# Forty-eight expert-routed tokens by indexed rows instead of thirty-two, in a transformer kernel that streams its weights

## The reference, cut to what matters

```
act = gelu(einsum('thkd,td->thk', u[ib], tb))
out = einsum('thk,thkd->td', gb * act, v[ib])      # u, v: 16384 x 2048
x   = x + out
```

## Time and profile before

| | |
|---|---|
| median of 3 runs (lowest, highest) | 3161.68 us (3159.88, 3164.09) |
| the profiled execution's own time | 3165.17 us |
| its span, first to last instruction | 3163.4 us |
| mean granted TensorE clock | 0.991 |

### The profile page before, as it was taken

The page is one execution under the profiler, slowest core; times in us unless marked ns, Lnnn a source line. Parts: engine busy times, 40 slices in busy tenths (PEclk is TensorE's granted clock), DMA queues, the critical chain, the costliest instruction groups (busy, mean ns, idle before and its releaser), DMA issues.

```text
span 3163.4 us, 49697 instructions
## 1 busy us (share of the span) xinstructions
PE 3065.3 (97%) x19428; PEld 2810.0 (89%) x19428; DVE 2239.1 (71%) x3268; ACT 1407.0 (44%) x1670; POOL 142.6 (5%) x168
## 2 busy tenths in 40 slices
PE   7999999999999999999999999999898999999998
PEld 7899889899999999999999999998787888888887
DVE  4766549998867888888888677687655646555564
ACT  4465443366434444444444445434444333333333
POOL 1000000000001101011111000000000000000000
PEclk9999999999999999999999999999999999999999
DMA  5443454456767888888888665544353555555553
GB/s 201 175 145 145 148 194 152 164 209 215 257 239 281 316 298 310 299 315 298 311 299 308 238 240 175 186 164 153 132 177 115 191 191 186 195 186 188 194 189 133
DMA packets 95836, 673.14 MB, mean 213 GB/s; under 512 B 11560, under 2 KB 11584, under 8 KB 15968
## 3 DMA queue, kind: packets, MB, share of 16 engines
q1 hardware_dynamic: 77472, 562.07, 49.2%
q0 software_dynamic: 16224, 94.72, 8.8%
q10 hardware_dynamic: 2016, 14.68, 1.2%
HBM read 652.48 MB, written 18.89 MB: 212 GB/s over the span
## 4 chain that ended last, share of the span: by engine, by line
PE 86%; DVE 10%; ACT 3%; issue 1%; DMA 0%; ACTq 0%; POOL 0%; DVEq 0%; SPq 0%
PE bank L1862 29%; PE bank L1863 15%; PE bank L1890 6%; PE bank L1892 6%; PE bank L1891 6%; PE bank L1840 6%; PE bank L1842 5%; PE bank L1841 5%; DVE w_lo L1085 4%; PE bank L1868 2%; ACT w_hi L653 1%; DVE pick_a L1502 1%; PE bank L1954 1%; PE bank L2154 1%; DVE tmp L1269 1%
## 5 line engine op out<-in xcount | busy, mean ns | idle before, releaser
L1085 DVE TENSOR_TENSOR w_lo<-raw,w_hi 128x2048 fp32r<-128x2048 f32 x532 | 1218.4, 2290 | 543.3 <-ACT w_hi L653 521.0
L1862 PE MATMUL bank<-a_both,w_hi 128*128 128x448 f32 (+1 forms) x3840 | 1259.1, 380 | 7.1 <-DVE a_both L1102 3.9
L1863 PE MATMUL bank<-a_both,w_lo 128*128 128x224 f32 (+1 forms) x4096 | 1060.8, 269 | 0.0
L1862 PEld LDWEIGHTS bank<-a_both,w_hi 128*128 128x128 f32 x3840 | 721.7, 188 | 90.6 <-DVE a_both L1102 4.4
L1863 PEld LDWEIGHTS bank<-a_both,w_lo 128*128 128x128 f32 x4096 | 778.5, 190 | 11.7
L653 ACT ACTIVATE w_hi<-raw 128x2048 fp32r<-128x2048 f32 x308 | 588.4, 1911 | 395.0 <-PE bank L1892 376.9
L1840 PE MATMUL bank<-a_both,w_hi 128*128 128x256 f32 (+1 forms) x1984 | 572.0, 288 | 21.2 <-DVE w_lo L1085 14.0
L666 ACT ACTIVATE w_hi<-raw 128x1536 fp32r<-128x1536 f32 x224 | 333.6, 1489 | 571.4 <-PE bank L1863 570.0
L1841 PE MATMUL bank<-a_both,w_hi 128*128 128x256 f32 (+1 forms) x1984 | 560.1, 282 | 0.0
L1842 PE MATMUL bank<-a_both,w_lo 128*128 128x256 f32 (+1 forms) x1984 | 559.9, 282 | 0.0
L1840 PEld LDWEIGHTS bank<-a_both,w_hi 128*128 128x128 f32 x1984 | 383.8, 193 | 28.8 <-issue 12.3
(11 more groups left out here) (326 smaller groups left out, 2442.0 us busy)
## 6 DMA issues: line engine op xcount, KB each, us to landing
raw<-stream_dram SPq DMA_DIRECT2D x532, 1024.0 KB
gates_scratch<-stage ACTq DMA_DIRECT2D x14, 1024.0 KB, 4.8
gbuf<-gates_scratch POOLq DMA_DIRECT2D x30, 448.0 KB, 7.0
x<-x_dram SPq DMA_DIRECT2D x2, 1024.0 KB, 6.6
x_scratch<-x POOLq DMA_DIRECT2D x1, 2048.0 KB, 11.0
wide<-wide_dram POOLq DMA_DIRECT2D x2, 1024.0 KB, 8.8
mem<-mem_dram POOLq DMA_DIRECT2D x1, 2048.0 KB, 9.5
xm<-x_scratch POOLq DMA_DIRECT2D x1, 2048.0 KB, 9.5
```

Source lines behind the costliest of these rows:

```text
L1085: eng.tensor_tensor(w_lo[k % SPLIT][:, :], raw[:, k % RAW, :], w_hi[k % SPLIT][:, :].bitcast(F32), ALU.subtract).then_inc(split_done, 1)
L1862: mm(o, hi[:, ks], pair, start=kt == 0, stop=False)
L1863: inst = mm(o2, lo[:, ks], pair[:, 0, :], start=False, stop=False, skip_group_check=True)
```

## The change: what it does

G becomes 48, in two sets: tokens 0 to 31 as before, and tokens 32 to 47 as eight groups of 16, so that 16 more tiles of each kind are fetched (`SETS`). The dense columns TD become 208, the gate groups 52, the gate blocks 13. There are 96 gathers and jobs in place of 64, 18 in a full round in place of 13, up to u7. The tokens' rows are multiplied by the norm's weights once, early (48 partitions, in the projection wq), stored to DRAM, and laid out for both sets by two DMAs. In rounds 2 to 7 the rounding of the gated product moves from DVE to ACT (`cast`), and the last piece of it on DVE (`act_lo`) is done one unit later. The second selection matmuls stand in e7, the norm of the memory input is later, and its tiles are turned at units 5 to 15 of e7, two at a time at first (`GMEM_AT`). The indices, gates and factors of the rows are laid out by 36 small DMAs in place of 12.

```diff
-G = 32
-GROUPS_G, GJ = P // G, PICKS // (P // G)
+SETS = [(0, 32), (32, 16)]
+G = GJ = sum(n for _, n in SETS)
+SET_DMAS = sum(P // n for _, n in SETS)
 TD = T - G
...
-        JOBS_U, JOBS_E = (1, 4, 7, 10, 13), tuple(range(0, 16, 2))
+        JOBS = {"u": (1, 3, 5, 6, 8, 10, 11, 13), "e": (0, 2, 3, 5, 6, 8, 10, 11, 13, 14)}
+        JOBS_FIRST = (3, 5, 6, 8, 9, 11, 12, 13)
+        JOBS_LAST = (1, 3, 5, 7, 9, 11)
...
+        GMEM_AT = {5 + j: (2 * j, 2 * j + 1) for j in range(5)}
+        GMEM_AT.update({10 + j: (10 + j,) for j in range(6)})
...
             eng.wait_ge(s_xd, 16)
+            eng.wait_ge(tr_done, TRQ["ln2"] + 16)
+            eng.dma_start(wide2[0:G, :], wide_in[2:3, :].partition_broadcast(G)).then_inc(s_wide2, 16)
+            eng.wait_ge(xw_done, 1)
+            eng.dma_start(xw_d, xw[0:G, :]).then_inc(s_xw, 16)
...
             gather(0)
-            eng.dma_start(wide2[:, :], wide_in[2:3, :].partition_broadcast(P)).then_inc(s_rows, 16)
+            gather(1)
             eng.wait_ge(mm_done, UNIT0["u2"])
-            for c in range(GROUPS_G):
-                eng.dma_start(h_rows[c * G:c * G + G, :], x_d[0:G, :]).then_inc(s_rows, 16)
-            eng.wait_ge(rows_done, 1)
-            gather(1)
+            for i, (t0, n) in enumerate(SETS):
+                src = bass.AP(tensor=xw_d.tensor, offset=t0 * D, ap=[[0, P // n], [D, n], [1, D]])
+                eng.dma_start(set_rows[i][:, :], src).then_inc(s_rows, 16)
...
+            def cast(r, k):
+                eng.wait_ge(g_used, 16 * r + k + 1)
+                eng.activation(a2[0][:, k, 0:TD], tmp[:, k % 4, 0:TD], ACT.Copy).then_inc(act_hi, 1)
...
                     eng.activation(tmp[:, j, 0:TD], tmp[:, j, 0:TD], ACT.Gelu).then_inc(tmp_full, 1)
+                    if k >= 1:
+                        cast(r, k - 1)
                     if k == 15:
                         ahead_rest(u)
+                        cast(r, 15)
...
+                if s == 2:
+                    eng.wait_ge(s_wide2, 16)
+                    eng.tensor_tensor(xw[0:G, :], x[0:G, 0, :], wide2[0:G, :], ALU.mult).then_inc(xw_done, 1)
...
-            def gating(r, k):
+            def gate_hidden(r, k):
...
-                own.do(eng.tensor_copy(a2[0][:, k, 0:TD], t))
-                eng.tensor_tensor(a2[1][:, k, 0:TD], t, a2[0][:, k, 0:TD].bitcast(F32), ALU.subtract).then_inc(tmp_split, 1)
+            def act_lo(r, k):
+                eng.wait_ge(act_hi, 16 * (r - 2) + k + 1)
+                eng.tensor_tensor(a2[1][:, k, 0:TD], tmp[:, k % 4, 0:TD], a2[0][:, k, 0:TD].bitcast(F32), ALU.subtract)\
+                    .then_inc(tmp_split, 1)
...
-                    gating(r, k)
+                    gate_hidden(r, k)
+                    if k > 0:
+                        act_lo(r, k - 1)
                     if k == 15:
+                        act_lo(r, 15)
                         ahead(UNIT0[f"u{r}"] + k)
-                    if (r, k) == (2, 1):
-                        eng.wait_ge(s_rows, 16 * (1 + GROUPS_G))
-                        eng.tensor_tensor(h_rows[:, :], h_rows[:, :], wide2[:, :], ALU.mult).then_inc(rows_done, 1)
...
             for j in range(16):
-                if j == 0:
-                    eng.wait_ge(sel_added, 1)
+                if j in (0, 1):
+                    sel_rows(1, j)
+                if j == 5:
+                    eng.wait_ge(sel_added, 2)
                     eng.wait_ge(normed, 4)
-                    turn_tile("gmem", mem, 0)
-                if j < 15:
-                    turn_tile("gmem", mem, j + 1)
+                for kt in GMEM_AT.get(j, ()):
+                    turn_tile("gmem", mem, kt)
```

More of the change, by code:

```diff
@@ L260, in build @@
         got = at("got", [P, 2, D], F32, work_at)
+        xw = at("xw", [P, D], F32, work_at)
         wide2 = at("wide2", [P, D], F32, work_at + 8192)
-        h_rows = at("h_rows", [P, D], F32, pk)
-        acc_rows = at("acc_rows", [P, D], F32, pk)
+        rows_at = work_at + 16384 + 4 * TBLOCKS * 4 * TBLOCK * 4
+        set_rows = [at(f"set_rows{i}", [P, D], F32, rows_at + 8192 * i) for i in range(len(SETS))]
+        assert rows_at + 8192 * len(SETS) <= work_at + WORK
         xm = at("xm", [P, TT, D], F32, work_at + 16384)
@@ L438, in build @@
         PART = 3 * UNIT // 4
-        JOBS_U, JOBS_E = (1, 4, 7, 10, 13), tuple(range(0, 16, 2))
+        JOBS = {"u": (1, 3, 5, 6, 8, 10, 11, 13), "e": (0, 2, 3, 5, 6, 8, 10, 11, 13, 14)}
+        JOBS_FIRST = (3, 5, 6, 8, 9, 11, 12, 13)
+        JOBS_LAST = (1, 3, 5, 7, 9, 11)
         JOB_AT, _n = {}, 0
-        for _r in range(2, PEER_ROUNDS - 1):
-            for _kind, _ks in (("u", JOBS_U), ("e", JOBS_E)):
-                for _k in _ks:
+        for _r in range(2, PEER_ROUNDS):
+            for _kind in "ue":
+                for _k in JOBS_LAST if _r == PEER_ROUNDS - 1 else JOBS_FIRST if (_kind, _r) == ("u", 2) else JOBS[_kind]:
                     if _n < 2 * GJ:
@@ L448, in build, with set_of @@
         assert _n == 2 * GJ
+        def set_of(j):
+            return next(i for i, (t0, n) in enumerate(SETS) if t0 <= j < t0 + n)
+        GMEM_AT = {5 + j: (2 * j, 2 * j + 1) for j in range(5)}
+        GMEM_AT.update({10 + j: (10 + j,) for j in range(6)})
         ROW_ACT_AT = next(at for at, n in JOB_AT.items() if n == GJ)
@@ L960, in _ @@
                 ahead_rest(UNIT0["e7"] + j)
+                if j < TT:
+                    eng.wait_ge(sel_done, 1)
+                    eng.wait_ge(s_mem, 16)
+                    square("gmem", mem, j)
             part_square(1, xm, 2)
@@ L1669, in _ @@
             for j in range(16):
-                if j == 0:
-                    scaled_lo("gmem", 0)
-                if j < 15:
-                    scaled_lo("gmem", j + 1)
+                for kt in GMEM_AT.get(j, ()):
+                    scaled_lo("gmem", kt)
                 accumulate(7, j)
                 ahead(UNIT0["e7"] + j)
+                if j == 2:
+                    sel_add(1)
+                    normalise("gmem", mem, mem)
                 if j in (6, 10, 14):
@@ L2179, in _, with sel_rows @@
                 feature("e2", 16, a2_both, r, unit=part_unit, rb=EB, c1=TD, ready=gated_tile("u2", r))
-            def sel_rows(h):
+            def sel_rows(i, h):
+                t0, n = SETS[i]
                 if h == 0:
-                    eng.wait_ge(got_used, 2 * GJ)
+                    eng.wait_ge(got_used, GJ + t0 + n)
                 for kt in range(8 * h, 8 * h + 8):
-                    last = mm(bank[4][:, kt * G:kt * G + G], acc_rows[:, kt * P:kt * P + P], C("sel"), start=True, stop=True)
+                    last = mm(bank[(4, 6)[i]][:, kt * n:kt * n + n], set_rows[i][:, kt * P:kt * P + P], C("sel", t0, t0 + n),
+                              start=True, stop=True)
                 if h == 1:
@@ L2403, in _constants @@
         np.broadcast_to(np.arange(P, dtype=np.float32), (P, P)),
-        (p % G == np.arange(G)[None, :]).astype(np.float32)], axis=1)
+        *[(p % n == np.arange(n)[None, :]).astype(np.float32) for _, n in SETS]], axis=1)
     onehot = np.zeros((BUCKETS, REL), np.float32)
```

90 lines of the change are left out of this document (48 added, 42 removed).

## The result

| | before | after |
|---|---|---|
| median us (lowest, highest) | 3161.86 (3159.88, 3164.09) | 3140.78 (3139.25, 3141.73) |
| ratio after / before, 95% interval | | 0.993 (0.9918 to 0.9942) |
| span of the profiled execution, mean granted clock | 3163.4, 0.991 | 3139.9, 0.989 |

A forecast was written before the change was run, and what follows sets the result against it. TensorE's own matmul sequence was taken as the bound, with VectorE and the DMAs next. 47.8 - 5.4 + 3.5 + 5.5 - 3.4 = 48.0 us saved, from 3161.7 to 3113.7 us (said as 3114), range 3090 to 3141.

The forecast's parts named there:

- The failed step: Small DMAs and row layouts: 24 more small DMAs and two layouts, issued while POOL is idle, were costed at nothing.
- such signs: Prediction wrong if the clock drops in the rounds or jobs wait for tiles; no w_hi was to wait for raw.
- Term 1, columns: In 224 units of e0, e1 and rounds 2 to 7, fewer w_hi columns save 47.8 us; w_lo sits at a floor.
- Term 2, VectorE: In rounds, TensorE waits for VectorE behind neighbouring jobs (3 us) and at changes from u to e (2.4): 5.4 lost.
- Term 3, the clock and the old stall: In u2, the 1.77 us wait for w_lo and 1.7 us lost at a lower clock go: 3.5 us saved.
- Term 4, gates: In u1, four groups fewer make units 11 and 12 shorter: 5.5 us saved, between 3 and 8.
- Term 5, selection: 16 more selection matmuls, two records each, 32 x 0.106: 3.4 us lost.
- the early multiplication: In wq, 2.2 us of VectorE falls into its idle 4.35 us: nothing; up to 5 if weights load late.
- 1 (no floor): In the matmul pairs all 48 columns count, giving 3090 to 3096 us; chance 0.2.
- 2 (the DMAs): In the rounds DMAs become the bound; at 340 GB/s sustained 30 us go back, 3144 us; chance 0.08.
- 3 (15 to 35 us given back by lag and late tiles): Longer VectorE lag, late tiles or the e7 shift give 15 to 35 us back, 3125 to 3150; chance 0.13.
- 4 (clock drop at every wait): In the rounds each wait throws the clock to its lower level, 66 us lost, 3175 us; chance 0.08.

The follow-up runs named there:

- e7: Not a run: a stage of the kernel, the e stage of round 7; 1.4 us longer in the changed kernel's trace than before.
- b_twelve: The changed kernel with the two row layouts loaded by twelve plain DMAs (four of 32 rows, eight of 16); 3124.2 us, ratio 0.9871.
- f_lo: b_twelve with the w_lo matmul taking only the first 104 of 208 columns in the 224 paired units; 3122.01 us, ratio 0.9873.
- f_hi: b_twelve with the w_hi matmul taking 400 of its 416 columns in the same 224 units; 3104.12 us, ratio 0.9815.
- c_copies: The changed kernel with multiplied rows written twelve times during wq, each layout then one DMA of 128 different rows; 3122.53 us, ratio 0.9878.
- m_wide0: The changed kernel with set 1 laid out by eight DMAs of 16 rows, set 0 still by one repeating DMA; 3148.4 us, ratio 0.9951.
- s_spaced: b_twelve with jobs moved to avoid neighbouring u units (7 in a u stage, 11 in an e stage); 3118.79 us, ratio 0.9862.
- v_cast: b_twelve with the rounding of the gated product back on VectorE, the subtraction directly behind it; 3131.74 us, ratio 0.9898.
- e6: Not a run: a stage of the kernel, the e stage of round 6; 1.9 us shorter in the changed kernel's trace than before.

## Why the prediction was wrong, point by point

**The failed step** is the sentence "the 24 more small DMAs and two row layouts are issued while POOL is idle", costed at nothing. It is true, and it prices the wrong thing: I looked at the queue that issues and not at the 16 engines that carry, nor at the first job, which waits for the layouts with a `w_lo` behind it. POOL was idle; the layouts then took 40.4 us, `w_hi` waited 14.5 us for the stream, VectorE 12.1 us for the rows, TensorE therefore 15.0 us for `w_lo`, and some 9.4 us went by at half the clock. The prediction had named such signs: the clock dropped in the rounds, `w_hi` waited for `raw`, and a job waited, though for its rows and not for its tile. b_twelve, which changes nothing else, gives 18.7 us back by the ratios and 17.7 by the spans, 19.6 of it in u2. The trace of before had no such DMA: its four loads of `h_rows` landed quickly, and one DMA with a leading repeat of 4 is another thing than four DMAs. That was to be bounded from both sides, and wasn't. The rest of the miss, 27 - 19 = 8 us, is spread over the small terms below. That 3140.8 lies just inside the stated range of 3090 to 3141 is luck: its high end was set for the DMA bound and for longer waits in all rounds, and neither came.

**Term 1, columns (47.8).** The number was nearly right, its reason was not. Pairs take 0.300 us, there are 1072 matmuls in the window of e0 and e1 (1067 said), and f_lo and f_hi show that the narrow matmul's columns are free and the wide one's are paid. But the prediction put the floor under the distance from `w_lo` to `w_hi`, and called itself wrong if that fell below 0.10: it fell from 0.101 to 0.095 in e1 (medians), the other distance from 0.212 to 0.205, and in f_lo it fell to 0.05. So neither the 0.106 us of the selection rows nor the 107 ns beside it is a floor for that distance; what the narrow matmul's columns hide behind is open. In u stages the unit stays near 4.85 us, not 4.80, 0.8 us a stage or 5 us over u2 to u7. That is in the traces; why is open. In u0, where I took nothing, it came out 0.9 us slower; in c_copies and m_wide0 it takes 96.8 us as before, so that comes and goes.

**Term 2, VectorE (-5.4).** Right in kind and place; the waits at the change from u to e have the predicted size, those behind neighbouring jobs a third of it. With a job VectorE's u unit took 5.50 us (5.57 said), its e unit 5.11 (5.15 said). The wait at the change from u3 to e3 (0.4 said):

```profile
1203.35 0.45 PE L1902 MATMUL bank<-a_both,w_hi 128*128 128x416 f32 x1 [0.34 <-DVE w_lo L1117]
```

There is one such at each change from u to e, 0.33 to 0.34 us long and 0.51 at e2, as the late subtraction makes it. Behind neighbouring jobs in u3 to u6 TensorE loses 0.11 us each time, in two pairs of 0.33 to 0.43 and 0.38 us instead of 0.30; 0.3 was said. The sum that gave 0.26 took 5.57 us twice, and twice 0.07 less leaves 0.12. s_spaced ends these; v_cast ends the waits at e3 to e6 and makes those behind neighbouring jobs 0.7 to 0.9 us long. Of b_twelve's two waits in the window 1100 to 1260 one, of 0.29 us, is of another kind: it stands behind a job of e2 whose tile came late:

```profile
1099.69 2.29 DVE L1635 CUSTOM_DVE_ANT_0 got<-got,set_rows 128x2048 f32<-128x2048 f32 x1 [1.16 <-DMA got<-u_rows_dram,row_idx]
```

Moving the cast is worth 8 us: without it VectorE would have been the next bound.

**Term 3, the clock and the old stall (+3.5)** can be judged by b_twelve alone, where u2 has neither: it takes 79.94 us, 5.3 less than before, where columns (3.4), stall (3.5) and waits (some -0.5) made 6.4. **Term 4, gates (+5.5):** u1 is 6.2 us shorter. Units 11 and 12 end 16.97 us after unit 10's, 15.1 said and 23.0 before:

```profile
757.96 0.34 ACT L927 ACTIVATE act<-bank 128x208 f32<-128x208 f32 x1 [0.19 <-PE bank L1882]
769.57 0.34 ACT L927 ACTIVATE act<-bank 128x208 f32<-128x208 f32 x1 [2.74 <-PE bank L1882]
774.93 0.34 ACT L927 ACTIVATE act<-bank 128x208 f32<-128x208 f32 x1 [3.21 <-PE bank L1882]
```

**Term 5, selection (-3.4):** the first set of 16 matmuls takes 1.70 us as before; e7 is 1.4 us longer than before, where columns and selection should have cancelled. TensorE waits in it once, 0.8 us for `a_both` (L1134) while it turns the memory norm's tiles, and not at all before; no run took the rest apart.

**Costed at nothing and right:** the early multiplication. wq is 1.5 us shorter, in all these kernels alike, and it stands in a gap of VectorE:

```profile
459.93 2.29 DVE L1117 TENSOR_TENSOR w_lo<-raw,w_hi 128x2048 fp32r<-128x2048 f32 x1 [3.47 <-ACT w_hi L674]
462.14 2.27 DVE L1480 TENSOR_TENSOR xw<-x,wide 48x2048 f32<-48x2048 f32 x1
```

The gathers landed after 7.8 us in the median and 11.4 at most (5.6 and 9.8 before), and no job of the change waited for one; b_twelve has the one wait shown under term 2.

**The rivals.** 1 (no floor): refuted by f_lo. 2 (the DMAs): the rounds run at a share of 0.95 and 346 GB/s, and in 1100 to 1260 no `w_hi` waits for `raw`; refuted there, though 3144 was close by accident. 3 (15 to 35 us given back by lag and late tiles): the size is what came, the mechanism was not this one; what came late was `set_rows`. 4 (clock drop at every wait): refuted. The window 1100 to 1260 holds the wait above and its granted clock is 1.00, and so it was behind the 1.66 us of s_spaced. In u2, behind 4.71 and 10.31 us, it fell. Why it fell behind the 1.77 us of before and not behind 1.66 is open.

Outside the touched stages the two traces differ too (xbc -1.2, out2 +2.6 us). out2 comes and goes between the kernels above, which are alike there (107.0 to 110.2 us, 107.6 before), so it is no effect of this change. xbc takes 71.8 to 73.5 us in all of them and 74.6 in the one trace of before; whether that is chance is not shown. A start of the layouts before u2 was not tried: the place of `set_rows` belongs to e1's tiles until then.

## What to carry to other kernels

Price a DMA by the engines that it will run on, not by the queue that issues it: write its source and its destination so that the outermost dimension of both is a multiple of 16, and put a repeat inside or into DMAs of their own, never in front as a 4. A burst that is small in bytes (2 MB here) stalls a tight stream if it sits on a few of the engines. Ask too who waits for it: in an engine with a fixed order everything behind the waiting instruction is late as well, and that was the larger part of the wait here. In the profile the sign is a DMA share near one with a third of the usual GB/s, and a landing time many times the usual one. And for pairs of matmuls like these, columns taken off the wide one count, columns off the narrow one (208 to 104) do not.
